# Token sums of the first norm on ScalarE, its factor kept in PSUM, and activations placed 48 elements on in three stages

## What is computed

```python
h = jnp.concatenate([meta, x], axis=1)              # 528 tokens
n = _rms(h, norm_mix_w[l])                          # x * rsqrt(mean(x*x) + eps) * w
z = n @ w_in[l]
q, k, v, glu, g_att, g_conv = jnp.split(z, splits, axis=-1)
...
u = glu[..., :CONV_CH] * jax.nn.sigmoid(glu[..., CONV_CH:])
u = jax.nn.silu(_layernorm(_causal_dwconv(u, ...), ...))
y_conv = u @ w_conv_out[l]
m = jax.nn.sigmoid(g_att) * y_att + jax.nn.sigmoid(g_conv) * y_conv
h = h + m @ w_out[l]
n2 = _rms(h, norm_ffn_w[l])
up = _causal_dwconv(n2 @ w_up[l], ffn_dw_w[l], ffn_dw_b[l])
gate, val = jnp.split(up, 2, axis=-1)
h = h + (jax.nn.silu(gate) * val) @ w_down[l]
```

## Time and profile before

| | us |
|---|---|
| median of 3 runs | 1942.04 (1940.70 to 1942.61) |
| the profiled execution | 1940.59 |
| its span on the core | 1938.8 |
| TensorE busy in it | 1901.1 (98%) |
| VectorE, ScalarE, GpSimd busy | 1134.7, 633.7, 71.9 |
| mean granted TensorE clock | 0.992 |

### The profile page before, as it was taken

How to read it: one execution, slowest core, us unless ns; L and a number is a source line. 1 busy time by engine, 2 the same in 40 slices (tenths; PEclk the granted TensorE clock), 3 DMA queues, 4 the chain that set the end, 5 groups by cost and what they waited for, 6 DMA issues and landing times.

```text
span 1938.8 us, 30718 instructions
## 1 busy us (share of the span) xinstructions
PE 1901.1 (98%) x12205; PEld 1706.1 (88%) x12205; DVE 1134.7 (59%) x1558; ACT 633.7 (33%) x1102; POOL 71.9 (4%) x72
## 2 busy tenths in 40 slices
PE   6999999999999999999999999999999999999998
PEld 5999888889999989989888888888898888888888
DVE  6677897896556646556765555444256555544522
ACT  4224454455234323323522222222243222222222
POOL 2000101101000000000000000000000000000000
PEclk7999999999999999999999999999999999999999
DMA  4222211112322232222323232323223323233231
GB/s 131 93 87 66 66 43 65 65 43 66 109 87 87 87 108 87 87 87 70 95 85 98 77 96 87 108 87 99 97 66 98 98 76 97 87 99 96 87 108 44
DMA packets 159794, 165.89 MB, mean 86 GB/s; under 512 B 3032, under 2 KB 156129, under 8 KB 159730
## 3 DMA queue, kind: packets, MB, share of 16 engines
q1 hardware_dynamic: 157224, 160.73, 25.7%
q10 hardware_dynamic: 2186, 4.20, 0.7%
q0 software_dynamic: 320, 0.07, 0.0%
HBM read 162.88 MB, written 2.10 MB: 85 GB/s over the span
## 4 chain that ended last, share of the span: by engine, by line
PE 90%; DVE 5%; issue 3%; ACT 1%; POOL 0%; DVEq 0%; DMA 0%; POOLq 0%; ACTq 0%
PE acc L421 71%; PE acc L812 4%; PE acc L551 3%; PE acc L487 2%; PE tr L848 2%; PE acc L776 1%; PE sc L834 1%; DVE y L1473 1%; PE sc L593 1%; PE tr L834 1%; PE tr L624 0%; DVE ssum L1437 0%; PE tr L622 0%; PE sc L855 0%; PE sc L470 0%
## 5 line engine op out<-in xcount | busy, mean ns | idle before, releaser
L1384 DVE TENSOR_TENSOR w_lo<-raw,w_hi 128x2048 fp32r<-128x2048 f32 (+1 forms) x148 | 337.6, 2281 | 151.5 <-ACT w_hi L968 150.0
L968 ACT ACTIVATE w_hi<-raw 128x2048 fp32r<-128x2048 f32 x147 | 279.9, 1904 | 434.2 <-PE acc L421 428.9
L421 PE MATMUL acc<-s_lo,w_hi 128*128 128x512 f32 x848 | 333.1, 393 | 0.0
L421 PE MATMUL acc<-s_hi,w_lo 128*128 128x512 f32 x848 | 330.3, 389 | 0.0
L421 PE MATMUL acc<-s_hi,w_hi 128*128 128x512 f32 x848 | 330.1, 389 | 0.0
L421 PE MATMUL acc<-n_lo,w_hi 128*128 128x256 f32 (+3 forms) x1024 | 241.7, 307 | 3.7 <-DVE n_lo L1417 3.1
L421 PE MATMUL acc<-n_hi,w_hi 128*128 128x256 f32 (+3 forms) x1024 | 232.6, 298 | 0.0
L421 PE MATMUL acc<-n_hi,w_lo 128*128 128x256 f32 (+3 forms) x1024 | 232.3, 298 | 0.0
L421 PEld LDWEIGHTS acc<-s_hi,w_lo 128*128 128x128 f32 x848 | 159.2, 188 | 33.2
L421 PEld LDWEIGHTS acc<-s_hi,w_hi 128*128 128x128 f32 x848 | 159.3, 188 | 32.0
L421 PEld LDWEIGHTS acc<-s_lo,w_hi 128*128 128x128 f32 x848 | 159.3, 188 | 32.0
(11 more groups left out here) (299 smaller groups left out, 2887.1 us busy)
## 6 DMA issues: line engine op xcount, KB each, us to landing
raw<-in_w_in SPq DMA_DIRECT2D x92, 1024.0 KB, 5.3
raw<-in_w_up SPq DMA_DIRECT2D x22, 1024.0 KB, 5.1
raw<-in_w_out SPq DMA_DIRECT2D x20, 1024.0 KB, 5.1
raw<-in_w_down SPq DMA_DIRECT2D x8, 1024.0 KB, 5.1
raw<-in_w_conv_out SPq DMA_DIRECT2D x4, 1024.0 KB, 5.1
decay<-in_decay ACTq DMA_DIRECT2D x8, 512.0 KB, 5.3
raw<-in_w_down SPq DMA_DIRECT2D x4, 768.0 KB, 4.3
xs<-in_x SPq DMA_DIRECT2D x4, 512.0 KB, 4.8
```

The source lines that it names most:

```text
L421: last = pe.matmul(acc[jj][:, bank, at_:at_ + n], w[j][:, k, jj * P:(jj + 1) * P], x[:, k0 + k, c:c + n], start=start and k == 0 and p == ...
L968: act.activation(w_hi[j][:, 0:kt, :], raw[j][:, 0:kt, :], ACT.Copy).then_inc(hi_full[j], 1)
L1384: dve.tensor_tensor(w_lo[j][:, 0:kt, :], raw[j][:, 0:kt, :], w_hi[j][:, 0:kt, :].bitcast(fp32), ALU.subtract).then_inc(lo_full[j], 1)
```

## The change

In the prologue:

- ScalarE squares the tokens where they were loaded (`xs`, `xm`, with tokens on the partitions) and sums each token's squares in the same instruction (`accum_out`) into `head_ms[:, 0:5]`. VectorE makes `var` from it, between its copies of the third and the fourth x tile. The squares of the transposed tiles, the sums L1437, and the matmuls with ones L446 of this norm are gone.
- TensorE spreads the factor over the partitions into both banks of `sc`, so that the 528 factors lie one after the other, and VectorE's L1423 reads them there. The copy to `rb` is gone, and the later counts of `rb_full` are one less.
- The six parameter loads move from SP's queue to the head of ScalarE's, ahead of the squares, and the four lambda loads stand behind the squares. The nine vectors on GpSimd's queue go in another order, `norm_mix_w` first.

In three stages (the convolution's output, `w_out`, and feed-forward up) the activations are written and read from element 48 of their rows on, instead of from 0.

```diff
+C2 = 48
@@ sync
-            sp.dma_start(prow[:, 0, :], io["conv_dw_w"][0]...).then_inc(s["ld_par"], 16)
...
@@ tensor
-            pe.wait_ge(s["xsums"], NQT + 1)
-            token_sums(ST_MIX, [ssum], T1 - P)
-            pe.wait_ge(s["pt_done"], 2)
-            broadcast(ST_MIX, [tr], META)
+            pe.wait_ge(s["st_pow"], ST_MIX + 1)
+            pe.wait_ge(s["x_done"], NQT + 1)
+            pe.matmul(sc[:, 0, 512 - META:512], pw[0:META, NQT:NQT + 1].to_broadcast([META, P]),
+                      ident[0:META, 0:META], start=True, stop=True)
+            for q in range(NQT):
+                last = pe.matmul(sc[:, 1, q * P:(q + 1) * P], pw[:, q:q + 1].to_broadcast([P, P]), ident[:, :],
+                                 start=True, stop=True)
+            last.then_inc(s["st_bc"], 1)
...
-                    chunk(j, i + B_CO, i * 2 + 2 * B_CO + j, m_hi, u_lo, T2,
+                    chunk(j, i + B_CO, i * 2 + 2 * B_CO + j, m_hi, u_lo, T2, c0=C2,
...
-                    chunk(j, i + B_WO, i * 2 + 2 * B_WO + j, n_hi, n_lo, T2,
+                    chunk(j, i + B_WO, i * 2 + 2 * B_WO + j, n_hi, n_lo, T2, c0=C2,
...
-                    chunk(1, i + b0, i * 2 + f0 + 1, m_hi, m_lo, T2)
+                    chunk(1, i + b0, i * 2 + f0 + 1, m_hi, m_lo, T2, c0=C2)
@@ scalar
+            act.dma_start(prow[:, 0, :], io["conv_dw_w"][0]...).then_inc(s["ld_par"], 16)
...
+            for q in range(NQT):
+                act.wait_ge(ld_x[q], 16)
+                if q >= 2:
+                    act.wait_ge(s["xsq"], q - 1)
+                act.activation((sq, nf)[q % 2].rearrange("p a n -> p (a n)")[:, 0:D], xs[:, q, :], ACT.Square,
+                               accum_out=head_ms[:, q:q + 1]).then_inc(s["xsq"], 1)
+            act.wait_ge(ld_x[NQT], 16)
+            act.wait_ge(s["ms_one"], 1)
+            act.wait_ge(s["xsq"], NQT - 1)
+            act.activation(sq[0:META].rearrange("p a n -> p (a n)")[:, 0:D], xm[:, :], ACT.Square,
+                           accum_out=head_ms[0:META, NQT:NQT + 1]).then_inc(s["st_sum"], 1)
...
-            for q in range(NQT + 1):
...
-                act.activation((sq, nf)[q % 2]..., h[:, :, c:c + n], ACT.Square).then_inc(s["xsq_full"], 1)
             hi(0, 0, None)
-            act.wait_ge(s["st_bc"], 1)
-            act.activation(rb[:, 0, META:T1], tr[:, 0, :], ACT.Copy)
-            act.activation(rb[:, 0, 0:META], tr[:, 1, 0:META], ACT.Copy).then_inc(s["rb_full"], 1)
             round_n(0, T1)
...
-                act.activation(m_hi[:, t, 0:T2], sq[:, t % 2, 0:T2], ACT.Copy).then_inc(s["uh_full"], 1)
+                act.activation(m_hi[:, t, C2:C2 + T2], sq[:, t % 2, 0:T2], ACT.Copy).then_inc(s["uh_full"], 1)
@@ vector
+                factor = sc[:, :, :].rearrange("p a n -> p (a n)")[:, 512 - META:1024]
...
-                                             scalar=weight(t), in1=rb[:, 0, 0:width], op0=ALU.mult,
+                                             scalar=weight(t), in1=factor, op0=ALU.mult,
...
+            dve.memset(head_ms[:, NQT:NQT + 1], 1.0).then_inc(s["ms_one"], 1)
             for q in range(NQT + 1):
                 src = (sc, tr)[q % 2]
+                if q == NQT - 1:
+                    dve.wait_ge(s["st_sum"], 1)
+                    dve.tensor_scalar(var[:, 0:NQT + 1], head_ms[:, 0:NQT + 1], 1.0 / D, 1e-6, ALU.mult,
+                                      ALU.add).then_inc(s["st_var"], 1)
                 dve.wait_ge(s["x_full"], q + 1)
...
-                if q:
-                    x_sums(q - 1)
-            x_sums(NQT)
...
-            mean_square(BC_MIX, 5, 1.0 / D, 1e-6)
             lo(0, 0)
```

More of the change, by code:

```diff
@@ L338, in _ @@
             pool.memset(u[:, :, 0:PAD], 0.0).then_inc(s["pads_done"], 1)
+            order = (3, 0, 1, 2, 4, 5, 6, 7, 8)
             vectors = [io[n].rearrange("a (t p) -> (a t) p", p=P) for n in
@@ L345, in _ @@
             vectors.append(io["conv_w_2"].rearrange("l k (t p) -> (l k t) p", p=P))
[L346 to L350, removed]
+            at_row = [sum(v.shape[0] for v in vectors[:n]) for n in range(len(vectors))]
+            for n in order:
+                src = vectors[n]
+                pool.dma_start(prow[at_row[n]:at_row[n] + src.shape[0], 4, :], src).then_inc(s["ld_vec"], 16)
             pool.dma_start(freq[:, :], io["freq"]).then_inc(s["ld_freq"], 16)
@@ L710, in up_pair @@
                     for x, (jj, ks) in enumerate(steps_in_turn(KT)):
-                        step = tile(0, jj, i * 2 + f0, i + b0, m_hi, m_lo, T2, ready=None if jj else ("n_full", KT), part=ks)
+                        step = tile(0, jj, i * 2 + f0, i + b0, m_hi, m_lo, T2, ready=None if jj else ("n_full", KT), part=ks, c0=C2)
                         if ks[-1] == KT - 1:
@@ L999, in round_n @@
                     act.activation(n_hi[:, t, 0:width], nf[:, t % 2, 0:width], ACT.Copy).then_inc(s["nh_full"], 1)
+            act.dma_start(prow[:, 0, :], io["conv_dw_w"][0].rearrange("k (t p) -> (k t) p", p=P)[0:P]).then_inc(s["ld_par"], 16)
+            act.dma_start(prow[0:TAPS * 8 - P, 1, :],
+                         io["conv_dw_w"][0].rearrange("k (t p) -> (k t) p", p=P)[P:]).then_inc(s["ld_par"], 16)
+            ffw = io["ffn_dw_w"][0].rearrange("k (t p) -> (k t) p", p=P)
+            act.dma_start(prow[:, 2, :], ffw[0:P]).then_inc(s["ld_par"], 16)
@@ new lines, in _ @@
+            act.dma_start(prow[0:4, 3, :], ffw[P:]).then_inc(s["ld_par"], 16)
+            act.dma_start(prow[4:48, 3, :], io["ffn_dw_b"].rearrange("a (t p) -> (a t) p", p=P)).then_inc(s["ld_par"], 16)
+            act.dma_start(prow[48:49, 3, :], io["subln_w"]).then_inc(s["ld_par"], 16)
+            for q in range(NQT):
[4 more added lines that the diff above has]
+                               accum_out=head_ms[:, q:q + 1]).then_inc(s["xsq"], 1)
@@ L1168, in _ @@
                         act.wait_ge(evac[jj], f + 2)
-                        act.activation(one(m_hi[:, ds(t, 1), 0:T2]), one(h[:, ds(t, 1), OLD:]), ACT.Copy,
+                        act.activation(one(m_hi[:, ds(t, 1), C2:C2 + T2]), one(h[:, ds(t, 1), OLD:]), ACT.Copy,
                                        scale=par[:, ds(V_FFN + t, 1)]).then_inc(s["nh_full"], 1)
@@ L1409, in half_mean, with normalise @@
                                   ALU.add).then_inc(s["st_var"], 1)
[L1411 to L1413 removed]
+            def normalise(idx, weight, c0, width):
+                dve.wait_ge(s["st_bc"], 1)
+                factor = sc[:, :, :].rearrange("p a n -> p (a n)")[:, 512 - META:1024]
                 def rest(t):
@@ L1689, in _ @@
                         dve.wait_ge(s["nh_full"], t + (KT + 1))
-                        dve.scalar_tensor_tensor(out=one(m_lo[:, ds(t, 1), 0:T2]), in0=one(h[:, ds(t, 1), OLD:]),
-                                                 scalar=column(t + V_FFN), in1=one(m_hi[:, ds(t, 1), 0:T2]).bitcast(fp32),
+                        dve.scalar_tensor_tensor(out=one(m_lo[:, ds(t, 1), C2:C2 + T2]), in0=one(h[:, ds(t, 1), OLD:]),
+                                                 scalar=column(t + V_FFN), in1=one(m_hi[:, ds(t, 1), C2:C2 + T2]).bitcast(fp32),
                                                  op0=ALU.mult, op1=ALU.subtract).then_inc(s["n_full"], 1)
```

44 lines of the change are left out of this document (11 added, 33 removed).

## The result

| | before | after |
|---|---|---|
| median, us | 1941.37 (1939.40 to 1942.61, 4 runs) | 1925.93 (1924.28 to 1927.68, 4 runs) |
| ratio, 95% interval | | 0.9922 (0.9904 to 0.9939) |
| the profiled execution, its span | 1940.59, 1938.8 | 1927.68, 1925.9 |

The change makes the kernel faster by 15.4 us, where 27 were forecast. The predicted 1915.0 is 10.9 us too low, and the range of 1909 to 1933 holds the time. In the traces the prologue gave what was said (10.0 us); the 48 elements gave 6 us instead of 17.

What follows compares the result with a forecast made beforehand. Bound by a prologue of latencies, then some 1900 us of TensorE matmul spacing. Prologue 10.0 plus 48 elements 17.0 make 27.0 us, so 1942.0 becomes 1915.0 us; range 1909 to 1933.

Steps and rivals of the forecast that it cites:

- Prologue, 10.0 us: Before the first product: without the relay of engines the first norm instruction starts at 18.4 instead of 28.38 us.
- my upper bound: Prologue: parameter loads beside x delay it by at most 1.2 us, putting the norm at 19.2; 0.4 was taken.
- What was late next: First chunk: paced by VectorE, ending with `lo(1, 0)`, whose chain moves as a whole; a sooner clock rise brings nothing.
- 48 elements, 17.0 us: Convolution output, `w_out`, feed-forward up: shifted activations save 12.2 ns a pair over 1440 pairs, 17.6 less 0.6 for a wait.
- 113.5 for 256 columns and 0.8 more for 258: Three stages: matmul spacing in ns taken from L551, making 227.8 a pair, 12.2 less than before.
- The bounds 0 and 17.6: Three stages: gain in us, 0 by the row 14 elements on, 17.6 by L551; -17.6 if the shift hurts.
- Rival 1: Three stages: the operand's start doesn't matter, L551 is fast for another reason; only the prologue gains, 1932.0 us; chance 0.12.
- rival 2: Three stages: moving operand after the weights slows matmuls to 126 ns, 1949.6 us, chance 0.06; at half size 1940.8, 0.04.
- Rival 3: Three stages: the distance helps only one matmul of each pair, half of 17.0 us; 1923.5 us; chance 0.07.
- Rival 4: Prologue: gives half, as small transfers delay x or ScalarE's issues stall; norm at 23.4, whole 1920.0 us; chance 0.07.
- The clock's own scatter: At 442 to 445 us the clock drops to 0.50; it may not fall, or fall elsewhere, worth 3 us.
- The forecast's own 1909 to 1920: Whole kernel: the range in us of the main forecast without the rivals, given 0.64.

Runs made afterwards that it cites:

- w16: Kernel after with the three stages' activations back at element 0 and all weights placed 16 elements further on; 1944.38 us, 1.0016 of the kernel before.
- c0: Kernel after without the 48 elements, so the prologue's changes alone; 1930.50 us, 0.9943 of the kernel before.
- even3: Kernel after with both matmuls of each pair 256 columns wide in all three stages, the last two columns left out; 1919.34 us, 0.9885.
- even3b: The same kernel as even3, unchanged, measured and profiled a second time; 1917.50 us.

## Why the prediction was right and wrong

- **Prologue, 10.0 us: right, step by step.** Sums ready at 11.8 forecast, 12.24 measured; parameter transposes 13.3, 13.71; copies into `par` 15.0, 15.28; `lo(0, 0)` until 18.4, 18.53. The errors up to the sums are at two places and partly cancel (0.7 late, 0.3 early). x's last tile was held up by 1.1 us, not 0.4 (8.9 to 10.04), which is near my upper bound; and the fifth square overlaps the reading of the fourth's sum, so the two took 2.2 us, not 2.5. The sums' 0.4 us shrink to 0.1 at the norm. ScalarE's six issues took 0.36 to 0.69 us each and end at 3.65, its function table is there at 4.97 and the first square follows at once: the forecast's 5 us. The factor's PSUM read costs nothing, 0.77 us a tile as before.
- **What was late next** was named: `lo(1, 0)` ends the first chunk, and the sooner rise of the clock brought nothing beyond the 9.97 us.
- **48 elements, 17.0 us: the direction and what causes it (the distance) right, the size wrong.** The step that failed is the term "113.5 for 256 columns and 0.8 more for 258". The row was the right one: with 256 and 256 columns a stage can take 113.6. The 0.8 was wrong: a neighbour of 258 columns costs not its two columns but the fast pace (all three stages took about 117.8 in every profile that has it at -16), and 12.2 ns a pair became 4.4. A second part of the step was silent: that the fast pace, once possible, is kept. With 256 and 256 columns everywhere it came only in part: 115.1 to 117.8 ns by stage in one execution, 113.3 to 114.7 in the other. I had the material to doubt the 0.8: the rows I had of the chunks' form had 258 columns and lay at 0 and 14, the rows of 256 columns alone had the swapped form, and none at -16 had a width that isn't a multiple of 64. The bounds 0 and 17.6 were fine.
- **Rival 1** (the start doesn't matter) fell with 117.8, and **rival 2** with it. The Trainium skill (SBUF — State Buffer, "Who interferes with whom") gives the moving operand and the weight load a port each; 113.3 against 120 ns for the same instructions at other distances doesn't fit two reads that never meet, unless the cause lies elsewhere in the path. The runs show that the distance counts, not what the two reads share.
- **Rival 3** (one matmul of each pair) gives 1923.5, near the measured time, but not by its mechanism. Both kinds of spacing fell, from 121.7 to 118.5 ns behind the 256 columns and from 118.4 to 117.2 behind the 258, in a pattern of six that goes from 114 to 121.
- **Rival 4** fell: the delay of x was real and small.
- **The clock's own scatter** went against the forecast, 2.8 us in the profiled run. The profiles of these kernels have between none (`w16`) and three such drops behind the prologue, one each in the two with the old prologue. That is too few to say whether the new prologue makes them likelier; `c0`'s median, 11.6 us under the kernel before, leaves no room for much of a cost.
- **The range** of 1909 to 1933 holds 1925.93 by its upper part, which was there for rival 1, in which the 48 elements give nothing. The forecast's own 1909 to 1920 does not hold it.

## What to carry to other kernels

Where TensorE is the bound, read its pace from the starts of dense stretches, form by form, and compare forms that differ only in where their operands lie; the start of the moving operand against the stationary one's, modulo 256 bytes, moved 256-column float32r matmuls between 113.3 and 120 ns, pairs of 256 and 258 columns between 117.8 and 122.7 a matmul, and 512-column ones between 226.7 and 233.3. Before a pace is carried from one place to another, the widths of both matmuls in turn must be the same, not only the distance: two columns more took two thirds of the gain. And a pace seen in one profile may be one of two: read it in a second execution before counting on it. A distance is chosen per form: what was best for 256 columns was the worst tried for 512.

## What the runs showed of the hardware

- 256-column matmuls at a distance of -16 or +16 elements run at 113.3 to 113.6 or at 117.8 ns, for whole chunks or blocks, and the same stretch changes from one execution to the next (`w_out` 117.8 in `even3`, 113.3 in `even3b`). Where L551 and the layers' heads stood at -16 they kept the fast pace in every profile.
- With 16 stationary columns instead of 128, 256-column matmuls ran at 113.3 to 113.5 ns at 0, +16, 32 and -16.
- The cost of the distance is not a property of the pair of tiles but of the form: at -16, two times 256 columns take 227.2 ns and one time 512 takes 233.3; at 0 it is 240.0 and 226.7.
- GpSimd's power of 128x5 took 3.19 us before and 1.21 after, the same instruction. In the kernel before VectorE's `w_lo`, with two operands in SBUF, ran beside it (timeline):

```profile
21.85 2.28 DVE L1384 TENSOR_TENSOR w_lo<-raw,w_hi 128x2048 fp32r<-128x2048 f32 x1
```

It ended at 24.13 and the power 1.1 us later; after, VectorE was copying out of PSUM meanwhile. By the Trainium skill (SBUF — State Buffer, "Who interferes with whom") a VectorE instruction with two inputs in SBUF contends with GpSimd's reads, and both durations agree with GpSimd being held up until the other's end. No run takes that instruction away in the prologue, but the layer norm's power of 128x5, at 449 to 460 us, shows the same. In ten profiles `w_lo` began 0.03 to 0.08 us ahead of it, and it took 3.25 to 3.30 us; in the other four, the kernels before and after among them, `w_lo` began 0.37 to 0.52 us behind it, and it took 1.18. Here these are `c0` and the kernel after (timeline):

```profile
449.38 2.29 DVE L1390 TENSOR_TENSOR w_lo<-raw,w_hi 128x2048 fp32r<-128x2048 f32 x1
449.45 3.25 POOL L348 TENSOR_TENSOR pw<-var,minus_half 128x5 f32<-128x5 f32 x1 [18.62 <-DVE var L1409]
...
450.57 1.18 POOL L348 TENSOR_TENSOR pw<-var,minus_half 128x5 f32<-128x5 f32 x1 [19.61 <-DVE var L1409]
451.10 2.29 DVE L1390 TENSOR_TENSOR w_lo<-raw,w_hi 128x2048 fp32r<-128x2048 f32 x1 [0.60 <-ACT w_hi L965]
```

The first norm's power was off the chain after, so it didn't bear on the forecast, but it was 2 us of the 28.38 before.
